# A decoder step on one core: one gated one-hot of each quad on GpSimd, dense U blocks loaded a block sooner, ScalarE's scan without its wait for a clearing

## The reference, cut to what matters

```python
def block(xb):
    q = einsum('td,dc->tc', xb, wq).reshape(blk, PEER_HEADS, 2, PEER_DKEY // 2)
    s = einsum('thcd,hckd->thck', q, keys)
    s1, i1 = top_k(s[:, :, 0], 16); s2, i2 = top_k(s[:, :, 1], 16)
    ...
    top, pos = top_k(cand, 16)
    eidx = take_along_axis(cidx, pos, axis=-1)
    gate = softmax(top, axis=-1)
    hid = gelu(einsum('td,thkd->thk', xb, take(u, eidx, axis=0)))
    return einsum('thk,thkd->td', gate * hid, take(v, eidx, axis=0))
```

## Time and profile before

| | us |
|---|---|
| median of 3 runs | 3342.91 |
| lowest and highest | 3335.14, 3353.33 |
| the profiled execution's own time | 3345.81 |
| its span | 3344.0 |
| TensorE busy | 3085.7 (92%) |
| VectorE busy | 2541.6 (76%) |
| GpSimd busy | 1735.6 (52%) |
| ScalarE busy | 939.5 (28%) |

### The profile page before, as it was taken

The page is one execution under the profiler, slowest core; times in us unless marked ns, Lnnn a source line. Parts: engine busy times, 40 slices in busy tenths (PEclk is TensorE's granted clock), DMA queues, the critical chain, the costliest instruction groups (busy, mean ns, idle before and its releaser), DMA issues. The chain is left out here.

```text
span 3344.0 us, 42557 instructions
## 1 busy us (share of the span) xinstructions
PE 3085.7 (92%) x13815; PEld 2050.5 (61%) x13815; DVE 2541.6 (76%) x5397; ACT 939.5 (28%) x2148; POOL 1735.6 (52%) x1418
## 2 busy tenths in 40 slices
PE   9999999999988899888786659999999999999998
PEld 9998887887433333333344437777667766777765
DVE  7771053888689999999899967777777777877777
ACT  3112212665112112112378851111111111111112
POOL 3243131443266777676655546555555555565554
PEclk9999999999999999999998879999999999999999
DMA  4435466778799999999989999999999999999997
GB/s 154 106 75 194 162 209 213 248 267 290 264 320 359 384 352 372 364 375 361 343 322 337 341 355 376 391 388 396 383 395 391 383 386 374 393 404 387 390 377 270
DMA packets 388784, 1074.52 MB, mean 321 GB/s; under 512 B 58824, under 2 KB 148744, under 8 KB 382176
## 3 DMA queue, kind: packets, MB, share of 16 engines
q0 software_dynamic: 186624, 679.56, 53.9%
q1 hardware_dynamic: 151280, 311.91, 26.4%
q10 hardware_dynamic: 50672, 80.51, 6.5%
HBM read 978.59 MB, written 93.11 MB: 320 GB/s over the span
## 5 line engine op out<-in xcount | busy, mean ns | idle before, releaser
L1752 POOL DMA_INDIRECT ub<-in_peer_u,gix x640 | 702.9, 1098 | 708.8 <-DVE hid L2044 515.4
L2419 PE MATMUL PB<-vbd,wd 128*128 128x512 f32 x1536 | 684.0, 595 | 0.0
L2406 PE MATMUL PB<-xds,uts 128*128 128x384 f32 x3072 | 569.8, 340 | 0.0
L2406 PEld LDWEIGHTS PB<-xds,uts 128*128 128x128 f32 x3072 | 532.0, 189 | 0.5 <-issue 0.5
L1752 POOL DMA_INDIRECT vbf<-in_peer_v,gix x340 | 396.7, 1167 | 164.8 <-issue 98.9
L2419 PEld LDWEIGHTS PB<-vbd,wd 128*128 128x128 f32 x1536 | 283.8, 191 | 308.9 <-issue 308.9
L2001 DVE TENSOR_TENSOR uts<-PB,uts 128x512 fp32r<-128x512 f32 x256 | 176.0, 687 | 306.5 <-ACT uts L2221 306.3
L2451 PE MATMUL PB<-vbf,dg 128*64 128x512 f32 x1200 | 313.5, 644 | 98.3 <-DMA vbf<-in_peer_v,gixv 89.5
L1752 POOL DMA_INDIRECT vbf<-in_peer_v,gixv x300 | 339.8, 1133 | 117.1 <-issue 86.1
L2044 DVE CUSTOM_DVE_ANT_0 ub<-ub,x1g 128x1024 f32<-128x1024 f32 x257 | 312.8, 1221 | 39.8 <-DMA ub<-in_peer_u,gix 31.0
L2221 ACT CAST uts<-PB 128x512 fp32r<-128x512 f32 x256 | 149.9, 586 | 645.7 <-PE PB L2395 634.2
(11 more groups left out here) (443 smaller groups left out, 5107.0 us busy)
## 6 DMA issues: line engine op xcount, KB each, us to landing
vbd<-in_peer_v SPq DMA_DIRECT2D x128, 512.0 KB, 6.9
x1d<-in_peer_u SPq DMA_DIRECT2D x96, 512.0 KB, 9.1
gd_d<-stag ACTq DMA_DIRECT2D x12, 2048.0 KB, 10.2
gbd<-gd_d SPq DMA_DIRECT2D x16, 1536.0 KB, 18.3
ubd<-in_peer_u SPq DMA_DIRECT2D x32, 512.0 KB, 9.7
wtr<-in_w_tok SPq DMA_DIRECT2D x6, 2048.0 KB, 9.2
tok_d<-stg ACTq DMA_DIRECT2D x48, 256.0 KB, 2.0
rb_e<-rows_d SPq DMA_DIRECT2D x8, 1536.0 KB, 10.0
```

The costliest lines, as they stand in the source:

```text
L1752: pool.indirect_dma_start(out=buf, out_offset=None, in_=a[table], in_offset=bass.IndirectOffsetOnAxis(ap=index, axis=0)).then_inc(done, 16)
L2406: last = T.matmul(PB[:, 6, 0:TD], uts[:, b % 2, ul, k, :], xds[:, xl, k, :], start=(k, n) == (0, 0), stop=(k, n) == (KD - 1, 2))
L2419: last = T.matmul(PB[:, 2 * d + n, :], wd[:, b % 2, d * CH:(d + 1) * CH], vbd[b % 8][:, n * 512:(n + 1) * 512], start=b == 0, stop=b == NB ...
```

## The change

GpSimd writes the gated one-hot of token 0 of every quad, two slots behind `quad_slot(q)` in its own loop, behind the gathers of that slot, with the same waits as VectorE's (`pkc`, `gmm`), and counts `ohp`; VectorE's loop starts at token 1, so that it writes one gated one-hot in even quads and none in odd ones; TensorE waits for `ohp` too. SyncE issues the load of U block 4 ahead of its loop and U b + 5 in round b. The rounds of `load_x1g(4)`, `load_gix(4)`, the first three `load_xs` and the last group of loads move from b = 25, 33, 38 and 92 to b = 28, 37, 42 and 96 (gates are loaded in rounds 9, 17, 25, 33, 41 and so on). ScalarE no longer waits for `setup`; TensorE waits for it ahead of the product with `hT` instead.

```diff
--- before.py
+++ after.py
@@ -993,7 +993,6 @@
                 last.then_inc(s["pe_a"], 1)
                 free(pe, s["dve_c2"], i)
                 if i == 0:
-                    pe.wait_ge(s["setup"], 1)
                     pe.wait_ge(s["wqk"], 32)
                 for w, b, done in ((wmk, 6, "pe_bk"), (wmq, 4, "pe_b")):
                     for h in range(MH):
@@ -1027,6 +1026,7 @@
                 free(pe, s["dve_h"], i)
                 if i == 0:
                     pe.wait_ge(ss["y2"], 1)
+                    pe.wait_ge(s["setup"], 1)
                 for g in range(NG):
                     last = T.matmul(PB[:, 4 + g, :], cht[:, CT0 + g, :], hT[:, g * 512:(g + 1) * 512], start=True, stop=True)
                 last.then_inc(s["pe_ys"], 1)
@@ -1111,7 +1111,6 @@
                 S.copy(by_head(qs), turned(0))
                 S.activation(by_head(ks), turned(1), ACT.Copy, scale=DK ** -0.5).then_inc(ss["qkc"], 1)
 
-            act.wait_ge(s["setup"], 1)
             tokens_stored(act)
             for i, q in pairs():
                 act.wait_ge(s["pe_a"], i + 1)
@@ -1526,7 +1525,7 @@
 
         s = {n: sem("pk_" + n) for n in (
             "xr gl1 gl2 mixg stt var sq mulg x1 x1c x1st x1t x1tc xtst sco scc hf top0 exp0 pick pkst "
-            "x1a x1h x1hc sc0 sc0c iota iou passed ix0 dot gelu gate diag pv ax acc0 ysum yvar ysq ymul y stored "
+            "ohp x1a x1h x1hc sc0 sc0c iota iou passed ix0 dot gelu gate diag pv ax acc0 ysum yvar ysq ymul y stored "
             "xsr ends_mean ends_sum kept dist ohx pkl pkt pkc oh gmm gev xdl xdh xdlo ut utc utl g1 hgs ws g2 x1dl tr trc sgel gz go").split()}
         s_wp = [sem(f"w_scores{n}") for n in range(4)]
         s_mt = [sem(f"mixt{n}") for n in range(2)]
@@ -1707,27 +1706,28 @@
                     load_v(b)
                 load_g(0)
                 load_g(1)
+                load_u(4)
                 for b in range(NBLK):
-                    if b + 4 < NBLK:
-                        load_u(b + 4)
+                    if b + 5 < NBLK:
+                        load_u(b + 5)
                     if b + 7 < NBLK:
                         load_v(b + 7)
                     if b % 8 == 1 and 8 < b < NBLK - 8:
                         load_g(b // 8 + 1)
-                    if block_slot(b) <= 386 < block_slot(b + 1):
+                    if block_slot(b) <= 394 < block_slot(b + 1):
                         sp.wait_ge(s["dot"], 3 * CH)
                         sp.wait_ge(s["acc0"], 1)
                         load_x1g(4)
-                    if block_slot(b) <= 408 < block_slot(b + 1):
+                    if block_slot(b) <= 418 < block_slot(b + 1):
                         sp.wait_ge(s["ax"], by_dve(3 * CH))
                         load_gix(4)
-                    if block_slot(b) <= 420 < block_slot(b + 1):
+                    if block_slot(b) <= 430 < block_slot(b + 1):
                         sp.wait_ge(s["pick"], NP - 1)
                         sp.wait_ge(s["mixg"], 4 * NP - 3)
                         sp.wait_ge(s["x1st"], 16 * PICK[SAMPLE])
                         for n in range(3):
                             load_xs(n)
-                    if block_slot(b) <= 560 < block_slot(b + 1):
+                    if block_slot(b) <= 570 < block_slot(b + 1):
                         sp.wait_ge(s["dot"], 4 * CH)
                         sp.wait_ge(s["acc0"], 3)
                         load_xs(3)
@@ -1769,6 +1769,14 @@
                     pool.sem_inc(s["passed"], 1)
                     at = 64 * e + 8 * h + m
                     gather(vbf[:, v % NB, :], "peer_v", (gixv if v < PE_ROWS else gixu)[n][:, at:at + 1], s_v[v % NB])
+
+                def first_hot(q):
+                    d, t0 = 4 * q // CH, 4 * q % CH
+                    pool.wait_ge(s["pkc"], d + 1)
+                    free(pool, s["gmm"], q - 1)
+                    pool.sem_inc(s["passed"], 1)
+                    nc.gpsimd.tensor_scalar(oha[:, q % 2, 0, :], iof[:, :], it[:, d, 0, t0:t0 + 1], it[:, d, 2, t0:t0 + 1],
+                                            ALU.is_equal, ALU.mult).then_inc(s["ohp"], 1)
 
                 for t in range(SLOTS):
                     c, h, k = t // CH, t % CH // TOPK, t % TOPK
@@ -1788,6 +1796,9 @@
                         gather(ub[:, t % NB, :], "peer_u", ixs[:, t - U_SLOTS:t - U_SLOTS + 1], s_u[t % NB])
                     for v in v_issues(t):
                         gather_v(v)
+                    for q in range(GQ):
+                        if min(quad_slot(q) + 2, SLOTS - 1) == t:
+                            first_hot(q)
                     if t in (290, 292, 294, 296):
                         k = (t - 290) // 2
                         if k == 0:
@@ -1981,7 +1992,7 @@
                     d, t0 = 4 * q // CH, 4 * q % CH
                     dve.wait_ge(s["pkc"], d + 1)
                     free(dve, s["gmm"], q - 1)
-                    for x in range(on_dve(q)):
+                    for x in range(1, on_dve(q)):
                         V.scalar_tensor_tensor(oha[:, q % 2, x, :], iof[:, :], it[:, d, 0, t0 + x:t0 + x + 1],
                                                it[:, d, 2, t0 + x:t0 + x + 1].to_broadcast([P, P]), ALU.is_equal, ALU.mult)
                     V.tensor_tensor(ohb[:, q % 2, :, :], iof[:, :].unsqueeze(1).to_broadcast([P, 4, P]),
@@ -2487,6 +2498,7 @@
                         if quad_slot(m) + 1 == t:
                             pe.wait_ge(s["oh"], m + 1)
                             pe.wait_ge(s["ohx"], m + 1)
+                            pe.wait_ge(s["ohp"], m + 1)
                             if m < 2:
                                 pe.wait_ge(s["pkc"], ND)
                             else:
```

## The result

The changed kernel took 3394.18 us (median of 4 runs, 3390.36 to 3403.93), the kernel before 3345.97 us beside it. The ratio is 1.0158, 95% interval 1.0134 to 1.0182: **slower by 1.6%**, where 3325 us had been forecast, and above the whole range of 3306 to 3343. The profiled execution of the changed kernel took 3403.93 us, span 3402.1.

A forecast was written before the change was run, and what follows sets the result against it. It took TensorE to bound the dense stage and no engine to be full in the one-hot stretch. U loads -17.5, scan -1.6 and one-hots -1.4 took 3345.8 to 3325.3, said as 3325 us, range 3306 to 3343.

The forecast's parts named there:

- 128 elements come to 0.47 us: One-hot stretch: estimated length of GpSimd's new instruction, from its larger copies at 0.81 ns an element.
- GpSimd has the time: One-hot stretch: GpSimd can take the 96 instructions, as it waits 89.7 us for VectorE there.
- the V rows' price: One-hot stretch: GpSimd's wait for a quad delays gathers, 18 of 34 V pairs late by 50 us together; taken +6 us.
- half of those 11.5 us is nearest to what gets onto the path: One-hot stretch: TensorE's idle time absorbs most V-row lateness; half of its 11.5 us of V waits sets the price.
- the quads themselves will find the one-hot ready: One-hot stretch: GpSimd's one-hot was ready at least 2 us before TensorE's quad wherever laid out.
- the rival of 0.08: One-hot stretch: V rows become TensorE's wait, +43 us at full price, 3370 us; chance 0.08.
- Both of its signs: For the V-row rival: over 11.5 us of V waits at L2451, and a one-hot stretch of over 316 us.
- The interference, +4: One-hot stretch: GpSimd's instructions hold VectorE's two-input ones for 11 us, 36% of it on the path: +4 us.
- The rival by which VectorE is held by each instruction: One-hot stretch: VectorE held for each GpSimd instruction's whole length, 45 us, 16 on the path; 3337 us, chance 0.12.
- The relief, -11.4: One-hot stretch: VectorE loses 96 gated one-hots, 31.9 us busy, 36% of it on the path: -11.4 us.
- The U loads, -17.5: Dense stage: U loads asked for a block sooner, so all five TensorE waits for U blocks go: -17.5 us.
- The scan, -1.6: Scan's start: ScalarE no longer waits for VectorE's last clearing and starts 1.6 us sooner: -1.6 us.

The follow-up runs named there:

- e1: The change without GpSimd's one-hots: VectorE writes all gated ones, moved U loads and scan's start stay; 3338.41 us, 0.9936 of the kernel before.
- e3: The change with GpSimd's 96 instructions writing a spare tile, without waiting for TensorE's quad, and VectorE writing all gated one-hots; 1.0048 of the kernel before.
- e20: e3, but TensorE waits for GpSimd's spare instructions only at the last quad; 1.0046 of the kernel before.
- e15: e1 with the pairs of V gathers issued one slot earlier from slot 250 on; 0.9966 of the kernel before.
- e16: e3 with the pairs of V gathers issued one slot earlier from slot 250 on; 1.0045 of the kernel before.
- e19: e20 with the pairs of V gathers issued one slot earlier from slot 250 on; 1.0040 of the kernel before.
- e2: The change with GpSimd's waits kept but no instruction issued behind them, VectorE writing all gated one-hots; 1.0076 of the kernel before.
- e12: The whole change with GpSimd's one-hot one slot later in its order (quad's slot + 3); 1.0068 of the kernel before.
- e5: The change with a third buffer for GpSimd's one-hot, so that it waits for one quad earlier; 1.0074 of the kernel before.
- e6: The change with GpSimd's one-hots for the first two quads only, VectorE still leaving the first one out throughout; 0.9919 of the kernel before.
- e8: e3 with GpSimd's instruction for every second quad alone, 48 in place of 96; 0.9997 of the kernel before.
- e18: The same kernel as e1, measured a second time on another chip; 0.9950 of the kernel before.
- e13: e1 with each pair of V gathers issued one slot earlier everywhere; 0.9991 of the kernel before.
- e14: The kernel before with only ScalarE's and TensorE's wait for VectorE's clearing at the scan's start moved; 0.9990 of the kernel before.

## Why the prediction was wrong

**The step that failed first: "128 elements come to 0.47 us", and "GpSimd has the time".** The instruction measured 0.78 us at the least, 1.10 in the median and 1.43 in the mean. The line through two copies was carried down to an eighth of the smaller one, and to another operation, without an upper bound: one instruction of 1.20 us stood in those rows, and 96 of that length are 115 us. GpSimd had 114.5 us of idle time before its U gathers: full, by the rows that I had in front of me. (The trace of before has 113 us of waits over 0.35 us in the slots 252 to 319; the new instructions took 137.5.) A step was missing too: I priced the 96 instructions as interference with VectorE and never added them up against GpSimd's own time beyond that one sentence. Work alone: +1.1% over e1 (e3, e20), +0.8 and +0.7% over e15, their base with early V rows (e16, e19).

**The second: the V rows' price, "+6, bounds 0 and +50".** The mechanism was right and laid out in the right place: the wait for a quad holds the next gathers back, and V rows land late at L2451, now L2462. The laid-out lateness of 50 us was about what came: V waits rose by 43.4 us with the wait alone (e2 against e1), and from 11.5 to 61.3 us in the change. That the last two agree so well is in part luck, since the lay-out knew nothing of GpSimd's own late work. What failed was that TensorE's idle time would take most of it ("half of those 11.5 us is nearest to what gets onto the path"). TensorE's 57.1 us before quads were idle time that VectorE ended, and VectorE and ScalarE don't run ahead when TensorE is late: they wait for its quads to free their buffers (VectorE 14.6 us before and 76.5 in the change, ScalarE 26.7 and 72.8 before its `away` tiles). A wait inside such a ring moves the ring. The lay-out also held only once: it took the order of events of before, without asking what the next quad, later by then, does to GpSimd's next wait. Of the change's 2.2% about 0.9 hang on this place (e12 and e5 against the change), and the wait alone costs 1.4% (e2). Put together, the parts give the whole within what these runs can tell: 1.4 + 1.1 - 0.2 = 2.3% against 2.2, and in the stretch 44.5 + 31.4 - 10.4 = 65.5 us against 73.8 over e1.

**The third: "the quads themselves will find the one-hot ready".** With an instruction of 0.47 us it stood ready 2 us before on paper. In the change TensorE's idle time before quads that ended with GpSimd's one-hot was 26.1 us, the largest share of the three engines it waits for there. The runs without that wait (e20, e19) were no faster than those with it (e3, e16), so by itself it decides nothing once GpSimd is late.

**A term that was at nothing: TensorE's clock.** The sum had only waits. With the lower granted clock (0.81 for 0.88 over the stretch) TensorE's own work took 19.6 us longer, of the 68.7. In all 20 kernels busy time times mean granted clock comes to 197 to 205 us in this stretch (e1 228.1 x 0.88, e3 242.8 x 0.82, e2 237.2 x 0.83), while busy time alone goes from 218.9 us (e6) to 249.6 (e12). So of what the work alone cost over e1, 31.4 us, 14.7 are busy time and 16.7 idle; in e8 it is 7.3 and 7.2. The clock fell along with idle time in every one of these kernels, and no run parts the two.

**So the rival of 0.08 was the case**, "V rows become the wait", with more than its price at full: its 50 + 4 - 11.4 = +43 became +68.7 in the stretch. Both of its signs are there, V waits over 11.5 us and a stretch over 316, and the stretch moved by far more than the 15 us that I had named as proof of being wrong. What this rival lacked is GpSimd's own work, 31.4 us of stretch when alone (e3 against e1), and the clock.

**The interference, +4**: right in kind, wrong in direction. VectorE's dot product went from 1216 to 1229 ns and its wide one-hot from 706 to 727: 64 x 13 + 96 x 21 ns, 2.9 us, in all. The most that any run shows is 1289 ns for the dot product in e12, 5 us over the 70 slots. It is GpSimd's instruction that is held. Three of them in the changed kernel's trace, with the gather between the first two, and VectorE beside the last:

```profile
1712.95 0.81 POOL L1778 TENSOR_SCALAR oha<-iof,it 128x128 f32<-128x128 f32 x1
1713.94 1.02 POOL L1752 DMA_INDIRECT ub<-in_peer_u,gix  x1 [0.17 <-PE PB L2507]
1715.00 0.81 POOL L1778 TENSOR_SCALAR oha<-iof,it 128x128 f32<-128x128 f32 x1
1716.57 2.32 POOL L1778 TENSOR_SCALAR oha<-iof,it 128x128 f32<-128x128 f32 x1 [0.77 <-issue]
```
```profile
1716.48 0.69 DVE L1998 TENSOR_TENSOR ohb<-iof,it 128x512 f32<-128x512 f32 x1 [1.62 <-PE PB L2507]
1717.09 1.22 DVE L2055 CUSTOM_DVE_ANT_0 ub<-ub,x1gb 128x1024 f32<-128x1024 f32 x1
```

The 32 of the 96 that had less than 0.05 us of VectorE's dot products and one-hots beside them took 0.82 us in the mean, the 51 with 0.5 us or more of them 1.93. The rival by which VectorE is held by each instruction, at 45 us, is refuted.

**The relief, -11.4**: not contradicted (10.4 us of stretch in e6's profile, 0.2% in the medians), and never paid out in the change.

**The U loads, -17.5**: right in mechanism, and somewhat too large. Dense stage -14.9 in the change, -15.9 and -16.1 in e1 and e18, all against the one trace of before; on one chip, e13 with the change's loads took 1295.9 us and e14 without them 1306.3, which is -10.4; no wait for a U block, none behind the sample rows at block 48, which I had left as a possible 16 us. The window from 2300 us, at 97.09 before, is at 100.00. With the scan's term the forecast of e1 is -19.1 us, 0.57%; measured -0.64 and -0.50%. With the U term at 10 to 16 us, the close match of e1 is in part luck. **The scan, -1.6**: 2.1 us at its first copy. Further on nothing can be told: the second chunk starts at 596.7 to 600.3 us and slot 0 at 879.9 to 886.0 in the kernels that share this code, and before has 599.5 and 882.6.

The version that is faster than both kernels is e1: U loads a block sooner and the scan's start, no one-hot on GpSimd, 0.9936 and 0.9950.

## What to carry to other kernels

Before work is moved to an engine because it "waits 90 us", add up what it would then do in that stretch, with gaps between instructions, at an upper bound for the new instruction's length, and compare with the stretch: an engine that issues the gathers is needed on time, not on average: with half of the work and 62 us of waits left (e8), about half of the loss was still there. A wait put into a queue that issues transfers couples every transfer behind it to the one waited for; when that one in turn waits for a transfer, it is a ring, and idle time in a ring is no cushion. In an experiment that isolates work, take out everyone's wait for its result too: it took e20 and e19 to say what e16 couldn't. And where TensorE is made to wait, its granted clock is looked up too: here it was more than a quarter of the loss.
